# A 64-column low-part product ahead of the 128-column high-part product in the probabilities-times-values step

## The reference, cut to what matters

```python
def block(qb):
    ...
    s = jnp.where(m, s, -1e30)
    p_slc = jax.nn.softmax(s.reshape(*s.shape[:4], n_sel * SLC_BLOCK), axis=-1).reshape(s.shape)
    o_slc = jnp.einsum('bhgqnl,bhqnld->bqhgd', p_slc, v_g)
    ...
    p_win = jax.nn.softmax(jnp.where(mw, s, -1e30), axis=-1)
    o_win = jnp.einsum('bhgqk,bkhd->bqhgd', p_win, vw)
    g = lax.dynamic_slice_in_dim(gates, q0, Q_BLOCK, 1).astype(f32).reshape(
        B, Q_BLOCK, NSA_KV_HEADS, NSA_GROUP, N_BRANCH)
    o = g[..., 0:1] * o_cmp + g[..., 1:2] * o_slc + g[..., 2:3] * o_win
```

## Time and profile before

| | |
|---|---|
| median of three executions | 819.66 us (819.59 to 821.3) |
| span of the profiled execution, first to last instruction | 817.9 us |
| PE busy, share of the span | 98% |
| PE weight loads | 83% |
| DVE, ACT, POOL | 63%, 53%, 52% |
| attention stage, by the first and last L1376 | 390.5 to 601.6 us |
| PE's granted clock in that stage | 1.00 of full speed |

### The profile page before, as it was taken

One profiled execution on the slowest core, in us unless ns is written; L12 is line 12 of the kernel. 1 busy time (PEld: TensorE's weight loads), 2 busy tenths in 40 slices (PEclk: granted clock), 3 DMA queues, 4 the chain that ended last, 5 costly groups with the idle time before them and its releaser, 6 DMA issues.

```text
span 817.9 us, 12432 instructions
## 1 busy us (share of the span) xinstructions
PE 800.5 (98%) x4578; PEld 680.4 (83%) x4578; DVE 516.0 (63%) x1008; ACT 436.7 (53%) x910; POOL 427.1 (52%) x371
## 2 busy tenths in 40 slices
PE   7999999999999999999999999999999999999995
PEld 7878888888988888888888889889878888887884
DVE  3782459951861804576999999999970263435426
ACT  4601154222233014758999999999972534426424
POOL 3302126355041121567779989899735464553554
PEclk9999999999999999999999999999999999999998
DMA  9511111201111111263200000000048332222237
GB/s 297 128 53 45 33 49 39 53 26 52 28 50 41 26 44 35 77 159 72 65 1 1 2 1 1 1 1 1 2 169 319 85 97 90 91 91 77 91 119 240
DMA packets 39918, 58.36 MB, mean 71 GB/s; under 512 B 11281, under 2 KB 17713, under 8 KB 39858
## 3 DMA queue, kind: packets, MB, share of 16 engines
q1 hardware_dynamic: 39570, 56.52, 23.3%
q0 software_dynamic: 288, 1.05, 0.8%
HBM read 49.16 MB, written 5.25 MB: 67 GB/s over the span
## 4 chain that ended last, share of the span: by engine, by line
PE 84%; DVE 11%; ACT 2%; issue 1%; POOL 1%; DMA 0%; DVEq 0%; SPq 0%; ACTq 0%; POOLq 0%
PE psum L1060 45%; PE psum L1353 6%; PE psum L1331 3%; PE psum L1332 3%; PE psum L1175 3%; PE psum L1376 3%; PE psum L1377 3%; DVE gla_att L2189 2%; DVE pT_lo L2363 2%; DVE gla_b L2180 1%; DVE p_slc L2335 1%; PE psum L982 1%; PE psum L981 1%; PE psum L980 1%; PE psum L1086 1%
## 5 line engine op out<-in xcount | busy, mean ns | idle before, releaser
L1850 POOL TENSOR_TENSOR w_lo<-w_raw,w_hi 128x512 fp32r<-128x512 f32 x124 | 180.1, 1457 | 306.2 <-ACT w_hi L1499 305.7
L1499 ACT ACTIVATE w_hi<-w_raw 128x512 fp32r<-128x512 f32 x124 | 78.2, 634 | 307.5 <-PE psum L1060 294.1
L1060 PE MATMUL psum<-w_hi,xT_hi 128*128 128x512 f32 x256 | 100.8, 394 | 0.6 <-DVE gla_state_b L2239 0.6
L1060 PE MATMUL psum<-w_hi,xT_lo 128*128 128x512 f32 x256 | 99.7, 389 | 0.0
L1060 PE MATMUL psum<-w_lo,xT_hi 128*128 128x512 f32 x256 | 99.6, 389 | 0.0
L2363 DVE TENSOR_TENSOR pT_lo<-psum,pT_hi 128x512 fp32r<-128x512 f32 (+1 forms) x148 | 95.1, 656 | 6.0 <-ACT pT_hi L1719 3.0
L1910 POOL TENSOR_SCALAR p_slc<-p_slc,gate_over_sum 128x512 f32<-128x512 f32 (+7 forms) x60 | 95.5, 1606 | 1.3
L1719 ACT ACTIVATE pT_hi<-psum 128x512 fp32r<-128x512 f32 (+1 forms) x148 | 82.3, 572 | 8.6 <-PE psum L1353 6.7
L1331 PE MATMUL psum<-kT,qT_hi_lo 128*128 128x384 f32 (+3 forms) x192 | 66.8, 350 | 0.9 <-DVE neg_max L2335 0.7
L1332 PE MATMUL psum<-kT,qT_hi_lo 128*128 128x384 f32 (+3 forms) x192 | 60.6, 328 | 0.0
L1376 PE MATMUL psum<-pT_hi,v_hi_lo 128*128 128x512 f32 x132 | 59.5, 451 | 0.6 <-DVE pT_lo L2363 0.6
(11 more groups left out here) (305 smaller groups left out, 1964.4 us busy)
## 6 DMA issues: line engine op xcount, KB each, us to landing
w_raw<-in_w_in SPq DMA_DIRECT2D x56, 256.0 KB, 2.7
w_raw<-in_ple_gate SPq DMA_DIRECT2D x32, 256.0 KB, 2.5
w_raw<-in_w_out SPq DMA_DIRECT2D x30, 256.0 KB, 2.6
x_tok<-in_x SPq DMA_DIRECT2D x8, 512.0 KB, 6.4
h_tok<-in_x SPq DMA_DIRECT2D x8, 512.0 KB, 6.1
kT<-kT SPq DMA_DIRECT2D x12, 256.0 KB, 3.6
out<-h_tok SPq DMA_DIRECT2D x6, 512.0 KB, 5.5
w_raw<-in_ple_proj SPq DMA_DIRECT2D x8, 256.0 KB, 2.5
```

Source lines behind the costliest of these rows:

```text
L1060: mm = pe.matmul(out, lhs, rhs, start=(first and n == 0), stop=(final and n == 2))
L1499: act.activation(w_hi(i)[:, 0:w], w_in(i)[:, 0:w], ACT.Copy).then_inc(s_whi, 1)
L1850: pool.tensor_tensor(w_lo(i)[:, 0:w], w_in(i)[:, 0:w], w_hi(i)[:, 0:w].bitcast(F32), ALU.subtract).then_inc(s_wlo, 1)
```

## The change

The pair of products of a unit changes places, and the low-part product is made with the 64 high-value columns alone. The product of low probabilities with low values is no longer computed. In the planner the cost of *values* goes from 625 to 572, and with that number the whole order of the attention stage is searched anew; the semaphores and buffers are the same.

```diff
@@ -698,7 +698,7 @@
             ops["low", u] = "V", 418 if few else 686, s
             after["low", u] = [("high", u)] + [("gate_end", 3)] * (u < 4)
-            ops["values", u] = "P", 625, s
+            ops["values", u] = "P", 572, s
             after["values", u] = [("low", u), ("output", j - ORING), ("gate_z", j if j < ORING else 3)]
@@ -1373,8 +1373,8 @@
             v = VS[:, span(qt, br)[0] // P + i, br - 1, kv]
-            pe.matmul(out, v, PTh[:, u % 4], start=False, stop=False)
-            pe.matmul(out, v, PTl[:, u % 4], start=False, stop=last).then_inc(s_pv, 1)
+            pe.matmul(out[0:DH], v[:, 0:DH], PTl[:, u % 4], start=False, stop=False)
+            pe.matmul(out, v, PTh[:, u % 4], start=False, stop=last).then_inc(s_pv, 1)
```

## The result

The changed kernel took 823.5 us (median of 5 runs, 822.96 to 824.13), the kernel before 821.1 us (819.59 to 821.68, 5 runs, two of them new beside the three known at the prediction). The ratio is 1.0036, 95% interval 1.0024 to 1.0048, about 3 us. The forecast was 816.3 us, a gain of 3.4.

A forecast was written before the change was run, and what follows sets the result against it. The prediction took PE to bound attention from 420 us on, with DVE and ACT close behind. Of 5.5 us saved on loads 4.1 come through, less 0.7 for late engines, gain 3.4: 819.66 to 816.3 us, range 813.6 to 820.4.

The forecast's parts named there:

- The 64-column load: Attention stage's value products: the narrower load saves 52 ns at 105 uncovered places, 5.5 us of PE time.
- The count of the long form of L1376: Low-part product behind transposes: its long form, 474 ns in the middle, was read as the case of an uncovered load.
- The new order: Searched order of the attention stage: 0 beside 0.9 us already counted, bounds 1.6 us either way.
- at most 1.4 us: Planner's deduction of 53 ns at 27 places where PE does not get it: plan slightly too early over the attention stage.
- What is late next: Attention from 420 us on: DVE and ACT fill up, so 0.7 us of the saving reappears as PE waits.
- where it falls: Of 5.5 us, 4.8 lie in the stretch after 420 us that PE bounds; 4.1 us come through.
- The swap: Value products of a pair: low product first adds no wait and saves nothing, 0.
- The drain: Rival: each 64-column value product changes array mode and drains PE, giving 858 us; chance 0.13.
- No cheaper load: Rival: 64-column load not cheaper or not felt by PE, only the order changes; 819.7 us, give or take 1.6; chance 0.07.
- the plan overshoots: Rival: PE gets ahead of pT_lo and waits grow by more than the load saves; 821.7 us, chance 0.04.

The follow-up runs named there:

- e1: The kernel before with its order kept (price of values 625) and only the new pair of products put in: 820.03 us, ratio 0.9998 to the kernel before.
- e2: The changed kernel's order (price of values 572) with the old pair of products, against the kernel before: 824.48 us, ratio 1.0055.
- e3: The kernel before, order kept, with the low-part product first but still with 128 columns: 819.94 us, ratio 0.9999.
- e4: New products in the old order, with selected and window branch transposes given 64 stationary columns instead of 128: 820.97 us in one run.

## Why the prediction was wrong

- *The 64-column load: the step that failed.* The load did shorten by 53 ns, but the prediction held it to be uncovered at 105 places, "behind an instruction of 128 streamed columns or fewer". It is uncovered at 10 of them, and at 3 others where PE waited for `pT_lo`. I read the 0.11 us between L1376's load and the next as the load's own length; behind a transpose it is the transpose's. The term of 5.5 us was 0.7 us (13 x 0.05) at most, and e1, with 13 such places too, measures a ratio of 0.9998. A row was there to warn: the transposes' loads last 140 ns in the middle, 50 less than a product's, and yet they stand 0.11 us apart too. That was a hint that something other than the load sets the distance.
- *The count of the long form of L1376* (474 ns in the middle) was taken to count uncovered loads. After the change, the middle is 472 ns with a load half as wide. The length said nothing of the load.
- *The new order: the second failure.* I took 0, within 1.6 us either way. e2 measures +0.55%, about 4.5 us. The bound was made from PE's waits in the second stretch, though the first one, where DVE sets the pace, has as much to lose: DVE's 31.30 us fell to 28.47 (29.11 in e2, whose clock stays at 1.00 there). And "at most 1.4 us" for the wrong price counted 27 pairs; it was wrong at 119 of 132, 119 x 0.053 = 6.3 us of PE time that the planner believed in.
- *What is late next, where it falls:* with nothing saved on PE these steps had nothing to act on; no run tests them.
- *The swap:* right, e3 has 0.9999.
- *The drain (0.13):* did not come. L1376's 64-column loads are made under the product ahead as before, and e1 loses nothing. By "TensorEngine Tiling (Array Packing)" of the Trainium skill, Key Properties, a change of tiling mode drains the engine; the trace shows no such drain for the one-pass 64-column product, so it isn't such a change, or is none that costs.
- *No cheaper load (0.07)* had the right outcome on PE, "PE doesn't feel it", and *the plan overshoots (0.04)* the right sign, at 821.7 us. Its mechanism, PE running ahead and waiting more for `pT_lo`, is not what the traces show: PE's waits for DVE hardly grew, and DVE lost its time waiting for ACT. The runs show one case that neither rival names whole: the load is covered, so nothing is gained on PE, and the new order is worse. I gave the two 0.11 together.

How much of the changed kernel's 0.36% is the price and how much the draw stays open within the scatter: seed 3 with 625 is with seed 7 the best of seven draws (0.9998 and 1.0 against a mean of 1.0009), and the changed kernel's 1.0036 is about the mean of the seven draws with 572 (1.0034). By which mechanism a low price would make a worse order is not shown by any run; the 1.34 us at 395.43 are one place of one order.

## What to carry to other kernels

Two starts that lie 0.11 us apart do not say whether the load or the stream sets the distance; find a row in which only one of them differs before pricing a narrower load. A change that alters a cost in a planner is two changes, and here the searched order was the larger: compare several seeds with the old and the new cost, and keep the old order beside the new code. A cost that depends on the neighbour should not be taken off every operation of a kind.

## What the hardware showed unexpectedly

- A transpose that streams 128 columns takes PE 0.109 us, with a load of 128 or of 64 columns (e4), while a product L1332 that streams 128 leaves room only for half a load: 0.06 us with 64 columns behind it, 0.11 with 128.
- The clock: in the changed kernel's profile the granted clock is 0.50 of full speed, the 1.2 GHz level, between 398 and 400 us.

```profile
398.00:400.00 2.00, 2.00 (x12) 2.00 (x11) 1.89 (x7) 1.35 (x5) 2.00 (x3) 0.50 0.00 0
```

  PE had stood idle for 1.04 us before 396.27, as shown above, right after eight scores of 64 streamed columns. The dip isn't the cause of the loss: e2 has the same order, a clock of 1.00 in its 388 to 420 us, and is no faster. The changed kernel's four other executions took 822.96 to 824.13 us with a mean clock of 0.998, against 824.07 us and 0.995 of the one profiled.
